# In-projection on rows as they came: gains on w_in, roots on the results, identity products at the start

## The chip, the core and the metric

The kernel runs on one core of one Trainium2 chip. The core has five engines that run side by side: TensorE (PE in the profile; its weight loads are listed as PEld) multiplies matrices, VectorE (DVE), ScalarE (ACT) and GpSimd (POOL) work on elements, and SyncE (SP) only issues transfers. ACT and POOL can issue transfers too; their issues appear as ACTq and POOL rows, those of SyncE as SPq. The metric is the device time of one execution in microseconds; lower is better.

## What is computed

One encoder layer on 1024 tokens of width 1024, in float32. The part that matters here is its beginning:

```python
h = _rmsnorm(x, attn_norm[l])            # x * rsqrt(mean(x*x) + eps) * g
z = h @ w_in[l]                          # 1024 x 1024 times 1024 x 1968
zq, zk, zv, zgate, zg, zcq, zckv, zkpe = jnp.split(z, split_pts, axis=-1)
```

After it come a gated linear attention on zq, zk, zv, zgate with the output gate zg, a latent attention on zcq, zckv, zkpe, an output projection with residual, and an MLP with squared ReLU with residual.

## The kernel before, in words

Every large product is made of float32 operands that are split in two: a high part, rounded to the reduced type fp32r by a copy on ACT, and a low part, which is the value minus its high part. One product is then three matmuls, high by high, high by low and low by high (`split_product`). So each slice of w_in (128 of its 1024 rows, by one group of columns) is transferred into the ring `raw` of four buffers, copied to `wi_hi` by ACT (`in_high_part`), and subtracted into `wi_lo` by DVE (`first_low_part`, the first column group) or POOL (`in_low_part`, the others). Each block of 128 rows of x is transposed on PE against the identity (`norm_T`), copied to `a_hi` by ACT (`norm_hi`), and subtracted into `a_lo` by DVE (`norm_lo`).

The in-projection runs over four groups of columns, q = 0 to 3. Group 0 has 432 columns (latents and gate), groups 1 to 3 have 512 (v, g, and q with k). In each group the eight row blocks b run one after the other, and each takes eight slices k, so 24 matmuls into one of the PSUM banks 0 to 3 (`in_project`). The results leave through DVE (`tile_out`). In group 2, ACT first computes the tanh for the gate.

The norm stands before all of this. ACT sums the squares of a block (`x_square`), POOL makes the root (`x_rstd`), DVE multiplies the block in place by the root and by `gain`, the norm's weights spread over all partitions (`norm_x`, line L1214), and only then does PE transpose it. PE waits for that in `norm_T` (L1756 is its transpose).

The order on each engine is written out by hand, and each engine runs its own list in order. What matters of these lists:

- SP issues the first block of x, then for each slice of group 0 two transfers, one of 416 and one of 16 columns (L456, L461). From the fifth slice on it waits for the low part that frees the ring buffer. For the next group it issues six slices, then the stores of the group (`stores`), and then the last two slices (k = 6 and 7).
- ACT (L957 and on) issues the second block of x, squares block 0, copies slices 0 to 3, issues the third block, copies block 0's transposes, squares block 1, copies slices 4 to 7, issues the fourth block; then for each b it issues one more block, squares block b + 2 and copies the transposes of block b + 1.
- From group to group, ACT and POOL prepare slices 0 and 1 of the next group early, and slices 2 to 7 during the last block. `wi_hi` and `wi_lo` have ten places (`SLICES`), so these six become free one by one as PE passes the last block; in group 2, ACT takes them after the tanh of the last block.
- Between the blocks, `behind(s)` on each engine does the steps of the latent attention's preparation: sums (L914), root (L682), latents transposed (L1827), heads (m_uq, m_ukv), squares (L949), norms, rotary part, transposes of the heads (L1813) and their copies `q_stage` on ACT.

In the profile, most matmuls have the line L1741, most copies of ACT L850, and the low parts of POOL L693.

## Time and profile before

| | before |
|---|---|
| median of 3 runs | 1203.54 us |
| lowest and highest | 1200.26 and 1203.76 us |
| the profiled execution | 1200.04 us, span of its instructions 1198.3 us |
| PE busy | 1160.1 us, 97% of the span |
| DVE, ACT, POOL busy | 780.2, 473.7, 481.4 us |
| mean granted clock of TensorE | 0.991 |
| first product of the in-projection | 12.96 us after the span's start |
| PE waiting for others (view of waits), in all | some 34 us, the longest single wait 9.6 us, at the start |

PE is busy nearly all the time, so what moves the end is only what PE waits for, and how fast its clock is. The profiled execution is a little below the median; a difference of the change is worked out against its rows and put onto the median.

### The profile page before, as it was taken

The numbers are of one execution on the slowest core, as the hardware profiler recorded it, in microseconds if no ns is written. First come the engines' busy times: TensorE is split into PE (matmuls) and PEld (weight loads), VectorE is DVE, ScalarE is ACT, GpSimd is POOL, SyncE is SP. The second block draws the span as 40 slices with busy tenths as digits, with TensorE's granted clock in tenths as the row PEclk, the third lists the DMA queues.
The fourth block names the chain that finished last, engine by engine and source line by source line (L and its number), as shares of the span: only waits on it lengthen the run. The fifth ranks groups of instructions, "written<-read, shape, count | busy, mean of one in ns | idle before, by whom it ended". The sixth has DMA issues, their size and how long they took to land.

```text
span 1198.3 us, 15216 instructions
## 1 busy us (share of the span) xinstructions
PE 1160.1 (97%) x5586; PEld 944.4 (79%) x5586; DVE 780.2 (65%) x1012; ACT 473.7 (40%) x907; POOL 481.4 (40%) x365
## 2 busy tenths in 40 slices
PE   6999999989999999999999999999998999999998
PEld 5967677768878788887788888888876888888887
DVE  5454866535656665137668557865787888888963
ACT  5344534215545555125612233323424334443441
POOL 2442545210000114305844444445435556555652
PEclk9999999999999999999999999999998999999999
DMA  7331342264111103421354342331559785356642
GB/s 239 90 98 62 109 121 87 71 180 172 27 28 43 38 1 114 151 88 71 93 171 141 134 147 94 125 126 62 202 179 357 263 282 192 113 186 210 212 123 88
DMA packets 97353, 158.41 MB, mean 132 GB/s; under 512 B 9024, under 2 KB 38736, under 8 KB 97280
## 3 DMA queue, kind: packets, MB, share of 16 engines
q1 hardware_dynamic: 95728, 152.53, 38.6%
q10 hardware_dynamic: 1008, 3.67, 0.8%
q0 software_dynamic: 544, 1.24, 0.5%
q8 instruction: 45, 0.74, 0.3%
q14 instruction: 28, 0.23, 0.1%
HBM read 115.46 MB, written 41.94 MB: 131 GB/s over the span
## 4 chain that ended last, share of the span: by engine, by line
PE 84%; DVE 8%; issue 3%; ACT 2%; DMA 2%; POOL 1%; SPq 1%; ACTq 0%; DVEq 0%; POOLq 0%
PE ps L1741 79%; PE ps L1961 3%; DVE t_all L1515 1%; DVE g_cum L1305 1%; DVE t_new L1515 1%; PE ps L1756 1%; PE ps L1813 1%; DVE dr_lo L1515 1%; POOL wi_lo L693 1%; DMA gain<-in_attn_norm_dram 1%; DMA up_raw<-in_w_up_dram 1%; DMA r_raw<-in_w_down_dram 1%; ACT q_stage L850 0%; PE ps L1898 0%; DVE a_lo L1515 0%
## 5 line engine op out<-in xcount | busy, mean ns | idle before, releaser
L1741 PE MATMUL ps<-dr_hi,dl_hi 128*128 128x512 f32 x448 | 175.5, 392 | 4.1 <-DVE dr_lo L1515 4.1
L1741 PE MATMUL ps<-dr_hi,dl_lo 128*128 128x512 f32 x448 | 175.3, 391 | 0.0
L1741 PE MATMUL ps<-dr_lo,dl_hi 128*128 128x512 f32 x448 | 175.3, 391 | 0.0
L814 POOL TENSOR_TENSOR ua_lo<-up_raw,ua_hi 128x1024 fp32r<-128x1024 f32 x46 | 116.7, 2539 | 118.1 <-ACT ua_hi L850 118.1
L836 POOL TENSOR_TENSOR dl_lo<-l_raw,dl_hi 128x512 fp32r<-128x512 f32 x64 | 101.6, 1613 | 74.5 <-ACT dl_hi L850 74.0
L1741 PE MATMUL ps<-wi_hi,a_hi 128*128 128x512 f32 (+1 forms) x256 | 105.1, 411 | 3.5 <-POOL wi_lo L693 2.1
L1741 PEld LDWEIGHTS ps<-dr_hi,dl_hi 128*128 128x128 f32 x448 | 84.8, 189 | 22.9 <-issue 3.3
L1741 PE MATMUL ps<-a_hi,ua_hi 128*128 128x512 f32 x256 | 99.9, 390 | 2.0 <-ACT u_two L850 1.8
L836 POOL TENSOR_TENSOR dl_lo<-s_all,dl_hi 128x512 fp32r<-128x512 f32 x48 | 74.7, 1574 | 63.5 <-ACT dl_hi L850 62.6
L1741 PE MATMUL ps<-a_hi,ua_lo 128*128 128x512 f32 x256 | 99.6, 389 | 0.0
L1741 PE MATMUL ps<-a_lo,ua_hi 128*128 128x512 f32 x256 | 99.6, 389 | 0.0
L1741 PE MATMUL ps<-wi_hi,a_lo 128*128 128x512 f32 (+1 forms) x256 | 99.3, 388 | 0.0
L1741 PE MATMUL ps<-wi_lo,a_hi 128*128 128x512 f32 (+1 forms) x256 | 99.2, 388 | 0.0
L1741 PEld LDWEIGHTS ps<-dr_lo,dl_hi 128*128 128x128 f32 x448 | 84.7, 189 | 17.7
L1741 PEld LDWEIGHTS ps<-dr_hi,dl_lo 128*128 128x128 f32 x448 | 84.7, 189 | 17.6
L850 ACT ACTIVATE ua_hi<-up_raw 128x1024 fp32r<-128x1024 f32 x48 | 50.5, 1057 | 87.1 <-PE ps L1741 78.7
L1515 DVE TENSOR_TENSOR dr_lo<-r_raw,dr_hi 128x512 fp32r<-128x512 f32 x64 | 72.5, 1132 | 16.8 <-ACT dr_hi L850 16.7
L1741 PE MATMUL ps<-m_kT,m_qT 96*128 96x512 f32 (+3 forms) x192 | 77.2, 512 | 4.0 <-ACT m_p L1040 4.0
L1741 PE MATMUL ps<-tx_hi,ua_hi 128*128 128x512 f32 x192 | 75.5, 393 | 2.3 <-DVE u_three L1515 2.3
L1741 PE MATMUL ps<-tx_lo,ua_hi 128*128 128x512 f32 x192 | 75.4, 393 | 0.0
L1741 PE MATMUL ps<-tx_hi,ua_lo 128*128 128x512 f32 x192 | 75.2, 392 | 0.0
L850 ACT ACTIVATE dl_hi<-l_raw 128x512 fp32r<-128x512 f32 x64 | 39.8, 622 | 85.3 <-PE ps L1741 83.9
(221 smaller groups left out, 2470.7 us busy)
## 6 DMA issues: line engine op xcount, KB each, us to landing
r_raw<-in_w_down_dram SPq DMA_DIRECT2D x144, 256.0 KB, 3.5
hidden<-stage SPq DMA_DIRECT2D x72, 256.0 KB, 2.0
up_raw<-in_w_up_dram SPq DMA_DIRECT2D x16, 1024.0 KB, 5.6
l_raw<-hidden SPq DMA_DIRECT2D x64, 256.0 KB, 3.4
raw<-in_w_in_dram SPq DMA_DIRECT2D x24, 256.0 KB, 3.0
z_gla<-z_stage SPq DMA_DIRECT2D x16, 256.0 KB, 2.1
raw<-in_w_out_dram SPq DMA_DIRECT2D x16, 256.0 KB, 5.9
xs<-in_x_dram SPq DMA_DIRECT2D x8, 512.0 KB, 8.7
```

What stands on the lines that cost most here:

```text
L693: pool.tensor_tensor(wi_lo[:, n % SLICES, 0:width], raw[:, k % RING, 0:width], wi_hi[:, n % SLICES, 0:width].bitcast(F32), ALU.subtract).t ...
L814: pool.tensor_tensor(ua_lo[n % UP_RING][:, :, :], up_source(g, product), ua_hi[n % UP_RING][:, :, :].bitcast(F32), ALU.subtract).then_inc( ...
L836: pool.tensor_tensor(slot(dl_lo, t), left_source(t), slot(dl_hi, t).bitcast(F32), ALU.subtract).then_inc(dllo_done, 1)
L850: return act.activation(dst, src, ACT.Copy, scale=scale)
L1305: last = dve.tensor_tensor_scan(g_cum[:, t, blk], ones[:, :], g_log[:, t, blk], 0.0, ALU.mult, ALU.add)
L1515: return dve.tensor_tensor(out_, in0, in1, op)
L1741: return pe.matmul(dst, lhsT, rhs, start=start, stop=stop, skip_group_check=onto)
L1756: last = pe.transpose(bank4(4 + j)[:, i, :], src[:, (4 * j + i) * P:(4 * j + i + 1) * P], ident[:, :])
L1813: last = pe.transpose(bank4(4 + i // 4, DQK)[:, i % 4, :], m_qk[:, b % 2, i, :], ident[:, :])
L1961: last = pe.transpose(bank4(4 + c // 4)[:, c % 4, :], m_p[:, i % 2, c * P:(c + 1) * P], ident[:, :])
```

## The change

x is no longer multiplied before it is transposed. The product (x * root * g) @ w is made as root * (x @ (g * w)): the norm's weights multiply the rows of w_in, and the root multiplies each row of the result.

- `gain` spread over the partitions (512 KB) gives way to `gain_col`, 128 by 8, in which each partition has the weights of its own rows; its transfer is issued after the identity is made.
- In group 0, ACT's copy to `wi_hi` takes the weight as its scale, and DVE's low part becomes (raw * gain) - hi in one instruction. In groups 1 to 3, ACT first multiplies the slice in place, waits for that, and then copies it to `wi_hi`; POOL's subtraction is as before.
- DVE's eight `norm_x` go. PE's transposes wait for the block of x alone.
- `tile_out` multiplies by the root, in group 2 through `half_rstd` (half of the root), which also is the scale of the tanh; DVE makes it at the first block of group 1.
- On ACT, the start is reordered: the second block of x is issued only when the first has landed; slices 0 and 1 come first, then block 0's transposes, slices 2 and 3, the squares of block 0, slices 4 to 7, the squares of block 1. DVE's list follows it.
- PE begins with ten products of the identity with itself into bank 3: six before the transposes of block 0 and four behind them. In the first block, PE waits for the first half of `a_lo` before slice 0 and for the second before slice 4.
- Counts of `xn_ready` follow, and POOL's wait for it before four small transfers goes.

```diff
--- before.py
+++ after.py
@@ -36,6 +36,7 @@
 ZM = MLA_W + GR
 
 RING = 4
+WARM_UP = 10
 SLICES = 10
 FT = W // P
 IN_GROUPS, OUT_GROUPS = 4, NH
@@ -227,6 +228,8 @@
         c_rs = small("c_rs", [P, NB, 2])
         h_ss = small("h_ss", [P, 2 * MH])
         h_rs = small("h_rs", [P, 2 * MH])
+        gain_col = small("gain_col", [P, KT])
+        half_rstd = small("half_rstd", [P, NB])
         m_nm = small("m_nm", [P, 2])
         m_sum = small("m_sum", [P, 2, NB])
         m_rden = small("m_rden", [P, NB])
@@ -699,10 +702,10 @@
                 pool.wait_ge(ssq_ready, b + 1)
                 rsqrt(rstd[:, 0, b:b + 1], ssq[:, 0, b:b + 1], D, rstd_ready)
 
-            pool.dma_start(gain[:, :], attn_norm[0].partition_broadcast(P)).then_inc(gain_in, 16)
             step(pool.memset(ident[:, :], 0.0))
             pool.affine_select(out=ident[:, :], in_=ident[:, :], compare_op=ALU.not_equal, fill=1.0, base=0,
                                pattern=[[-1, P]], channel_multiplier=1).then_inc(ident_ready, 1)
+            pool.dma_start(gain_col[:, :], attn_norm[0].rearrange("(k p) -> p k", p=P)).then_inc(gain_in, 16)
             step(pool.memset(minus_half[:, :], -0.5))
             x_rstd(0)
             x_rstd(1)
@@ -722,7 +725,6 @@
             last.then_inc(freq_ready, 1)
             pool.memset(ones[:, :], 1.0).then_inc(ones_ready, 1)
 
-            pool.wait_ge(xn_ready, NB)
             pool.dma_start(gqk[:, 0, :], q_head_norm[0].partition_broadcast(P)).then_inc(phase_in, 16)
             pool.dma_start(gqk[:, 1, :], k_head_norm[0].partition_broadcast(P)).then_inc(phase_in, 16)
             pool.dma_start(gn[:, :], gla_out_norm[0].partition_broadcast(P)).then_inc(phase_in, 16)
@@ -860,7 +862,12 @@
                         act.wait_ge(z_ready, NB * (q0 + 1))
                     else:
                         act.wait_ge(slice_free, (KT - 1) * q0 + k0 + 1)
-                copy(wi_hi[:, n % SLICES, 0:width], raw[:, k % RING, 0:width]).then_inc(whi_done, 1)
+
+                if q:
+                    step(copy(raw[:, k % RING, 0:width], raw[:, k % RING, 0:width], gain_col[:, k:k + 1]))
+                    copy(wi_hi[:, n % SLICES, 0:width], raw[:, k % RING, 0:width]).then_inc(whi_done, 1)
+                else:
+                    copy(wi_hi[:, n % SLICES, 0:width], raw[:, k % RING, 0:width], gain_col[:, k:k + 1]).then_inc(whi_done, 1)
 
             def high_part(q, k):
                 act.wait_ge(raw_in[k % RING], raw_value(q, k))
@@ -955,16 +962,20 @@
                 if s == LOGITS + 2:
                     act.activation(g_cum[:, :, :], g_cum[:, :, :], ACT.Ln, bias=1.0).then_inc(softplus_ready, 1)
 
+            act.wait_ge(x_in[0], 16)
             x_load(1)
+            act.wait_ge(gain_in, 16)
+            for k in range(2):
+                in_high_part(0, k)
+            norm_hi(0, 0)
+            x_load(2)
+            for k in range(2, 4):
+                in_high_part(0, k)
             x_square(0)
-            for k in range(4):
-                in_high_part(0, k)
-            x_load(2)
-            norm_hi(0, 0)
-            x_square(1)
+            x_load(3)
             for k in range(4, KT):
                 in_high_part(0, k)
-            x_load(3)
+            x_square(1)
             for b in range(NB):
                 if b + 4 < NB:
                     x_load(b + 4)
@@ -986,7 +997,8 @@
                         act.wait_ge(z_ready, NB * q + b + 1)
                         if b >= 1:
                             act.wait_ge(z_out, NB * q + b)
-                        act.activation(tanh_g[:, :], ps[:, b % 4, :], ACT.Tanh, scale=0.5).then_inc(tanh_ready, 1)
+                        act.wait_ge(z_out, NB + 1)
+                        act.activation(tanh_g[:, :], ps[:, b % 4, :], ACT.Tanh, scale=half_rstd[:, b:b + 1]).then_inc(tanh_ready, 1)
                     if q + 1 < IN_GROUPS and b in (0, NB - 1):
                         for k in range(0, 2) if b == 0 else range(2, KT):
                             in_high_part(q + 1, k)
@@ -1110,7 +1122,7 @@
                 if n < UP_RING:
 
                     act.wait_ge(x2_stored[n], 32)
-                    act.wait_ge(xn_ready, NB + 2 * n + 2)
+                    act.wait_ge(xn_ready, 2 * n + 2)
                 else:
                     act.wait_ge(part_ready, 2 * (n - UP_RING + 1))
                 if product in (P1, P4):
@@ -1253,24 +1265,28 @@
                 q, b = divmod(s, NB)
                 dve.wait_ge(z_ready, s + 1)
                 tile = ps[:, s % 4, :]
+                root = rstd[:, 0, b:b + 1]
                 n = s - NB
                 if 2 <= n < 2 * NB:
                     dve.wait_ge(z_stored[n % 2], 16 * (n // 2))
                 if q == 0:
-                    dve.tensor_copy(zm[:, b, :], tile[:, 0:ZM]).then_inc(z_out, 1)
+                    dve.wait_ge(rstd_ready, b + 1)
+                    dve.tensor_scalar(zm[:, b, :], tile[:, 0:ZM], root, None, ALU.mult).then_inc(z_out, 1)
                 elif q == 1:
-                    dve.tensor_copy(z_stage[:, n % 2, :], tile).then_inc(z_out, 1)
+                    if b == 0:
+                        dve.tensor_scalar(half_rstd[:, :], rstd[:, 0, :], 0.5, None, ALU.mult)
+                    dve.tensor_scalar(z_stage[:, n % 2, :], tile, root, None, ALU.mult).then_inc(z_out, 1)
                 elif q == 2:
 
                     dve.wait_ge(phase_in, 64)
                     dve.wait_ge(tanh_ready, b + 1)
                     step(stt(z_stage[:, n % 2, :], tanh_g[:, :], 1.0, tile, ALU.add, ALU.mult))
                     g4 = z_stage[:, n % 2, :].rearrange("p (h v) -> p h v", h=GH)
-                    stt(g4, g4, 0.5, gn[:, :].unsqueeze(1).broadcast_to([P, GH, GDV]), ALU.mult, ALU.mult).then_inc(z_out, 1)
+                    stt(g4, g4, half_rstd[:, b:b + 1], gn[:, :].unsqueeze(1).broadcast_to([P, GH, GDV]), ALU.mult, ALU.mult).then_inc(z_out, 1)
                 else:
 
                     dve.wait_ge(cum_ready, GT)
-                    dve.tensor_copy(zqk[:, b, :], tile).then_inc(z_out, 1)
+                    dve.tensor_scalar(zqk[:, b, :], tile, root, None, ALU.mult).then_inc(z_out, 1)
 
             def head_norms(b):
 
@@ -1339,20 +1355,16 @@
 
             def first_low_part(k):
                 dve.wait_ge(whi_done, k + 1)
-                dve.tensor_tensor(wi_lo[:, k, 0:ZM], raw[:, k % RING, 0:ZM], wi_hi[:, k, 0:ZM].bitcast(F32),
-                                  ALU.subtract).then_inc(wlo_done, 1)
+                stt(wi_lo[:, k, 0:ZM], raw[:, k % RING, 0:ZM], gain_col[:, k:k + 1], wi_hi[:, k, 0:ZM].bitcast(F32),
+                    ALU.mult, ALU.subtract).then_inc(wlo_done, 1)
 
             dve.wait_ge(gain_in, 16)
-            norm_x(0, 0, x0, x0[:, 0, :])
-            for k in range(RING):
+            for k in range(2):
                 first_low_part(k)
             norm_lo(0, 0)
-            norm_x(0, 1, x0, x0[:, 1, :])
-            for k in range(RING, KT):
+            for k in range(2, KT):
                 first_low_part(k)
             for b in range(NB):
-                if b + 2 < NB:
-                    norm_x(0, b + 2, x0, x0[:, b + 2, :])
                 if b + 1 < NB:
                     norm_lo(0, b + 1)
                 tile_out(b)
@@ -1747,7 +1759,7 @@
                 return mm(dst, lo, rhs_hi, False, last, onto)
 
             def norm_T(r, b, src):
-                pe.wait_ge(xn_ready, NB * r + b + 1)
+                pe.wait_ge(x_in[b], 16)
                 for j in range(2):
                     n = 2 * (NB * r + b) + j
                     if n >= 2:
@@ -1763,6 +1775,8 @@
                 if n >= 4:
                     pe.wait_ge(z_out, n - 3)
                 for k in range(KT):
+                    if n == 0 and k % 4 == 0:
+                        pe.wait_ge(alo_done, k // 4 + 1)
                     if between is not None and k == KT // 2:
                         between()
                     if b == 0:
@@ -1862,11 +1876,16 @@
 
 
             pe.wait_ge(ident_ready, 1)
-            norm_T(0, 0, x0[:, 0, :])
+
+            for n in range(WARM_UP):
+                if n == WARM_UP - 4:
+                    norm_T(0, 0, x0[:, 0, :])
+                mm(ps[:, 3, 0:P], ident[:, :], ident[:, :], True, True)
             for b in range(NB):
                 if 1 <= b < NB - 1:
                     norm_T(0, b + 1, x0[:, b + 1, :])
-                pe.wait_ge(alo_done, 2 * b + 2)
+                if b:
+                    pe.wait_ge(alo_done, 2 * b + 2)
                 in_project(0, b, (lambda: norm_T(0, 1, x0[:, 1, :])) if b == 0 else None)
                 behind(b)
             for q in range(1, IN_GROUPS):
@@ -2021,7 +2040,7 @@
 
 
             def norm_T2(pos):
-                pe.wait_ge(xn_ready, NB + pos + 1)
+                pe.wait_ge(xn_ready, pos + 1)
                 if pos >= 2:
                     pe.wait_ge(xt_free, pos - 1)
                 elif pos == 0:
```

## Rows read from the trace of the kernel before

**Rows 1.** Timeline at the start: start us, duration us, engine, line, operation, out<-in, [idle before]

```profile
1.29 0.75 POOL L702 DMA_DIRECT2D gain<-in_attn_norm_dram  x1 [0.80 <-POOLq L2131]
2.52 0.29 POOL L704 TENSOR_SCALAR_AFFINE_SELECT ident<-ident 128x128 f32<-128x128 f32 x1 [0.25 <-POOL ident L703]
5.59 1.03 ACT L876 ACTIVATE ps<-x 128x1024 f32<-128x1024 f32 x1 [3.08 <-DMA x<-in_x_dram]
8.18 1.28 DVE L1214 SCALAR_TENSOR_TENSOR x<-x,rstd,gain 128x1024 f32<-128x1024 f32 x1 [8.18 <-DMA gain<-in_attn_norm_dram]
8.34 2.23 ACT L850 ACTIVATE wi_hi<-raw 128x432 fp32r<-128x432 f32 x4 [1.60 <-DMA raw<-in_w_in_dram]
```

**Rows 2.** Chain that ended last, in order of time: start us, length us, what

```profile
12.96 4.69 PE ps L1741 x12
22.52 4.71 PE ps L1741 x24
```

**Rows 3.** Busy time by stretch, PE alone: stretch, us, PE busy, granted clock, DMA share, GB/s

```profile
13.00:14.00 1.00, 1.00 (x3) 1.00 1.04 376
```

**Rows 4.** DMA issues of the first 30 us: KB each, us from issue to landing

```profile
gain<-in_attn_norm_dram POOLq DMA_DIRECT2D x1, 512.0 KB, 6.9
places<-in_positions_dram POOLq DMA_DIRECT2D x1, 4.0 KB, 3.1
```

**Rows 5.** Timeline between blocks 0 and 1 of group 0

```profile
13.22 0.64 SPq L461 DMA_DIRECT2D raw<-in_w_in_dram  x1
14.30 2.38 ACT L850 ACTIVATE wi_hi<-raw 128x432 fp32r<-128x432 f32 x4 [1.08 <-DMA raw<-in_w_in_dram]
17.04 1.03 ACT L876 ACTIVATE ps<-x 128x1024 f32<-128x1024 f32 x1 [0.36 <-issue]
20.34 1.28 DVE L1225 TENSOR_TENSOR a_lo<-ps,a_hi 128x512 fp32r<-128x512 f32 x2
```

**Rows 6.** PE's timeline: the latents' products, in plain float32

```profile
65.46 2.74 PE L1741 MATMUL ps<-m_uq,m_cT 128*128 128x384 f32 x8
```

**Rows 7.** PE's timeline after a long wait late in the kernel

```profile
875.75 0.67 PE L1741 MATMUL ps<-tx_hi,ua_hi 128*128 128x512 f32 x1 [2.26 <-DVE u_three L1515]
```

**Rows 8.** Busy time by stretch, PE alone, in the same place

```profile
875.00:880.00 5.00, 4.25 (x12) 0.66 0.83 276
```

**Rows 9.** Timelines of ACT, POOL and PE from group 0 to group 1

```profile
55.80 2.39 ACT L850 ACTIVATE wi_hi<-raw 128x512 fp32r<-128x512 f32 x4 [4.70 <-PE ps L1741]
56.51 7.54 POOL L693 TENSOR_TENSOR wi_lo<-raw,wi_hi 128x512 fp32r<-128x512 f32 x6 [4.57 <-ACT wi_hi L850]
62.00 0.63 ACT L850 ACTIVATE wi_hi<-raw 128x512 fp32r<-128x512 f32 x1 [0.84 <-DMA raw<-in_w_in_dram]
64.78 0.39 PE L1741 MATMUL ps<-wi_hi,a_hi 128*128 128x512 f32 x1
```

**Rows 10.** Timelines of DVE and PE after the first block of group 1

```profile
65.66 0.69 DVE L1262 COPY z_stage<-ps 128x512 f32<-128x512 f32 x1 [5.20 <-PE ps L1741]
77.22 0.52 PE L1827 MATMUL ps<-ident,zm 128*128 128x128 f32 x3 [1.82 <-ACT v_stage L850]
```

**Rows 11.** Groups of DVE, shapes apart: busy us, mean ns | idle before

```profile
L1326 DVE TENSOR_SCALAR g_log<-ps,bg 128x512 f32<-128x512 f32 x4 | 3.0, 750 | 0.3
```

**Rows 12.** Timelines of ACT and PE in the first blocks of group 2

```profile
148.37 1.30 ACT L850 ACTIVATE wi_hi<-raw 128x512 fp32r<-128x512 f32 x2 [0.68 <-DMA raw<-in_w_in_dram]
151.01 0.60 ACT L989 ACTIVATE tanh_g<-ps 128x512 f32<-128x512 f32 x1 [1.34 <-DVE z_stage L1214]
152.72 0.52 PE L1827 MATMUL ps<-ident,zm 128*128 128x128 f32 x3 [1.12 <-ACT q_stage L850]
```

**Rows 13.** Timelines of ACT, POOL and PE from group 2 to group 3

```profile
200.51 2.18 ACT L850 ACTIVATE wi_hi<-raw 128x512 fp32r<-128x512 f32 x4
201.21 7.99 POOL L693 TENSOR_TENSOR wi_lo<-raw,wi_hi 128x512 fp32r<-128x512 f32 x6 [2.19 <-ACT wi_hi L850]
209.25 0.50 PE L1741 MATMUL ps<-wi_hi,a_hi 128*128 128x512 f32 x1 [0.17 <-POOL wi_lo L693]
```

## The prediction, made before the change was run

> **What bounds the kernel now.** PE is busy 97% of the span, so I read the view of PE's waits first, for what it waits for at all, then the timelines of all engines at its longest wait, then the chain of work that ended last, which says which of those waits carry to the end. Everything the change touches lies in the first 210 us; the projections and the MLP behind it only move along with it.
>
> The longest wait is the first. The rows to see: the weights of the norm, spread over all partitions, are issued at 1.29 and let DVE start at 8.18 us [rows 1]; the first block of x had landed by 5.59. DVE's multiplication (1.28 us), PE's transposes, ACT's copy and DVE's low part follow one another, and the chain reaches the first product at 12.96 [rows 2]. The twelve products of 432 columns from there take 4.69 us, the 24 of the second block 4.71 [rows 2]: 0.39 against 0.20 us each. The granted-clock column reads 1.00 in that stretch [rows 3], but 432 columns in 0.39 us (with the first one's start-up) is the lower level, 1.2 GHz, and 0.20 the upper, 2.4, so I go by the distances here. The second block's products begin at 22.52 on the chain. From there on PE has work without a gap until the groups change, so **the change's worth at the start is the move of that 22.52**, not of 12.96.
>
> **The start, part by part.** Removed: 512 KB of spread weights, the 1.28 us of DVE, and the second block of x out of the first transfers, 1 MB of the 2.4 MB of the first transfers (two blocks of x, four slices, the weights). Added: gain_col, 4 KB in pieces of one element. The nearest row is the positions' transfer, the same 128 by 8 of four-byte values: 3.1 us to landing [rows 4]; the spread weights took 6.9. The identity is made first; it was ready at 2.52 + 0.29 = 2.81 behind an issue of 0.75 [rows 1], so at about 2.1 now, and gain_col is issued then: landed between 2.1 + 3.1 = 5.2 and 2.1 + 6.9 = 9.0. Slice 0 was complete at 8.34 [rows 1]; with 1 MB less at 376 GB/s [rows 3] it comes up to 2.8 us earlier, at 5.5. I take 6.2 as the time S at which ACT can start, near to the slice and to the positions' row, which is the same transfer; its end at 5.5 and, with half the distance to the spread weights' row, 7.4 bound this case, and 9.0 is a rival of its own below.
>
> From S in ACT's new order, with copies of 0.56 (2.23 / 4 [rows 1]) for slices and about 0.55 for transposes: slices 0, 1 to S + 1.1, both halves of block 0 to S + 2.2, one issue, slices 2, 3 to S + 3.7, DVE's low parts of 0.6 behind, the last at S + 4.4. The first product is at about S + 2.6 = 8.8, 4.2 us earlier than 12.96. But slice 7's buffer is freed by that last low part. Before, its last issue stood at 13.22, and its copy, the fourth of 2.38 us from 14.30, began by 16.1 and ended at 16.68 [rows 5]: 2.9 us from issue to copy at most. Now the last issue stands at about S + 5.2 (0.9 for the two), the copy begins at S + 8.1 and ends at S + 8.6 = 14.8.
>
> Behind slice 7 stands what I think decides: before, ACT had squared block 1 earlier; from 16.68 it issued two blocks, squared block 2 (17.04 [rows 5]) and copied block 1's transposes, DVE's low parts of these ended at 20.34 + 1.28 = 21.62 [rows 5], and the product came at 22.52, 0.9 later, with transposes between. Now the squares of block 1 stand in this line too. Counted: squares of block 1 and 2, 2 x 1.25 (1.03 [rows 5] and 0.2 for reading the sum); one issue 0.36; two halves 1.1; the last low part 0.8; then 0.9: 5.7 us. Block 1 starts at 14.8 + 5.7 = 20.5. **Gain 2.0 us**; with S at its bounds 2.7 and 0.8. Squares, roots (POOL) and x's later blocks are hidden: x's third block is issued at about S + 2.5 and isn't squared before S + 10.
>
> **The clock.** The ten identity products: the latents' float32 products show as eight rows of 384 columns in 2.74 us [rows 6], two rows for each matmul, so 0.69 us for 384 columns and 0.23 for 128 at full clock, 0.46 at half. Six cost 1.4 to 2.8 us from 2.1 on, over before or just as x lands; the other four end by 9 at the latest. They are covered by the wait for slice 0 and cost nothing; without that cover they would cost 2.3 to 4.6. They may well save the 0.19 us on each of the twelve slow products. But block 0 then waits for slices 4 to 7, which come no faster, so that saving isn't on the path: it is nothing of the sum. What counts is the clock when block 1 begins. Between the last product of block 0 (slice 7's low part, then three products: 14.8 + 1.3) and the next transposes (14.8 + 4.2) lie **2.9 us without work for PE, wherever S is**. The nearest row is the wait of 2.26 us before 875.75 [rows 7], behind which the granted clock averages 0.66 over 5 us [rows 8]: (1 - 0.66) / 0.5 x 5 = 3.4 us at the lower level, 1.7 us of work lost. Before, PE had no such gap here. Bounds: nothing if the clock holds, 2.8 if it comes back as slowly as at the start, where twelve products lost 12 x 0.19 = 2.3 us [rows 2] and the transposes behind them some more. I take **+1.7 us**, the nearest row's. The Trainium skill (TensorE: Matmul & The Clock Gate, "What's actually happening") says that the throttled state is the default and that activity lifts it, and in "HAM oscillation" that idle gaps between bursts bring it back: by the first the identity products pay, by the second the gap behind block 0 takes it back. The rows at the start and at 875.75 agree with each.
>
> **The changes of group.** In groups 1 to 3, each slice needs two passes of ACT instead of one, the second waiting for the first. The nearest rows: four copies in 2.39 us [rows 9], two in 1.30 [rows 12]; so 0.60 to 0.65 for a pass and 1.20 to 1.30 for the pair. POOL's low parts take 7.54 / 6 = 1.26 [rows 9] and 7.99 / 6 = 1.33 [rows 13]. So ACT becomes just as slow as POOL, and only the pair of the first slice and the second pass of the last stick out.
> - Group 0 to 1: POOL's last low part ended at 56.51 + 7.54 = 64.05; slice 7 came by transfer at 62.00 [rows 9]. Its buffer is free 0.6 later (the first pair), it lands 0.6 later, and its pair takes 0.6 more: low part at 65.3. PE wants it at 64.78 [rows 9]: +0.5.
> - First block of group 1: its result opens DVE's rotary steps (65.66 [rows 10]), at whose end PE waits 1.82 us (77.22 [rows 10]). half_rstd costs 0.2 and the multiplication 0.75 [rows 11] instead of 0.69: +0.3 on this path.
> - Group 1 to 2: the low parts are late here for another reason (DVE and POOL behind the scans), so the pairs hide up to slice 7. But behind it, ACT's heads are 0.65 later, so their store, so the two next slices that SP issues behind it (148.37 [rows 12]); with their two pairs ACT is free at about 151.6 and not before the tanh at 151.01, for whose q_stage PE waits 1.12 us (152.72 [rows 12]): +0.65, bounds 0 and 1.4.
> - Group 2 to 3: ACT starts at 200.51, POOL at 201.21, and PE waits for the last, 209.25 [rows 13]. First pair and second pass of the last: +1.1, and ACT's next copies for PE +0.15; bounds 0.65 and 1.5.
> - The other results of DVE: 24 times 0.06 us and POOL's freed wait are hidden; PE has four banks.
>
> Sum of these: +2.7, bounds 1 and 4. The whole: -2.0 + 1.7 + 2.7 = **+2.4 us**. The profiled execution's own 1200.04 becomes 1202.4; it lies 3.5 below the median, and against the median of 1203.54 the forecast is **1205.9**.
>
> **The rivals.**
> - The clock holds over the gap. For it: PE is not quite idle before it, and the identity products end close to the first product. Then -2.0 + 2.7 = +0.7: 1204.2.
> - Faster: the start pays in full. gain_col lands at 5.2, ACT's pairs hide behind POOL except at one change of group, and the clock holds: -2.7 + 1.0 = -1.7. If slice 7's copy also comes 2 to 3 us sooner after the start than before, -4 to -5: 1198.5 to 1201.8. Against it: slice 7 hangs on the ring, not on traffic.
> - Slower: ACT becomes the bound at the changes of group. It decides as soon as a pair takes longer than POOL's 1.26 to 1.33. At 1.5 us, five more slices at two changes cost 0.2 each, +2.0; at 1.6, +3.0: with the clock lost, 1207.9 to 1208.9. At 1.3 or less, none of it. For it: two full passes with a wait between are at that edge already.
> - gain_col as the new wait, as the first product was held by gain before. One element for each piece; at 6.9 us as the spread weights, S is 9.0, and block 1 starts at 23.3 instead of 22.52, so +0.8 in place of -2.0: 1208.7. The Trainium skill (DMA: Bandwidth & Descriptors, "Rules for kernel authors") says of a non-contiguous last dimension that it is one descriptor per element and should be rearranged; that speaks for this one. The positions' row at 3.1 us speaks against it.
> - The identity products don't raise the clock. Then block 0 runs at half; its last product comes later, the gap shrinks, and block 1 starts up to 1 us later: 1204.5 to 1206.9, inside the range.
>
> **How the numbers follow.** Forecast with the clock lost 0.37; clock holds 0.24; faster 0.18; ACT as the bound 0.11; gain_col late 0.05; identity without effect 0.05. A measurement of this kernel can tell about 0.3% from no change, 3.6 us: below 1199.9 or above 1207.2. Faster by that is most of the third case: 0.14. Slower by that: the fourth and fifth cases and the upper part of the first, 0.24. The same: 0.62. The range goes from 1199.5, inside the faster rival, to the slower one's 1208.9.
>
> **What would show it.** In the profile after: PE's first rows are identity products at about 2; ACT's first copy ends its wait at 5.6 to 7.4, and what released it says whether gain_col or slice 0 was last; the first product near 8.8; the copy of slice 7 ends near 14.8; block 1's first product at 20.5 by my count, with a gap of about 2.9 us before its transposes, and products at 0.36 (432 columns at 1.2 GHz) instead of 0.20 us behind it if the clock went. ACT's pairs at 1.2 to 1.3 us; POOL's last low part of groups 1 and 3 about 1.1 us later against the block it follows. What would make it wrong: slice 7 landing well before S + 8, a clock that stays up, or pairs longer than 1.35 us.

## The result

The changed kernel takes 1208.8 us (median of 7, 1206.0 to 1211.1) where the kernel before, on the same chip, takes 1200.9 (median of 7): a ratio of 1.0065 with an interval of 1.0047 to 1.0083, so **7.8 us slower**. The forecast was slower by 2.4; the time lies at the upper end of the range, and the sign of the sum was right, but its size was a third of what happened. That the time lies inside the range is luck: the forecast was put onto a median of three runs, 1203.5, and the seven here have 1200.9. As a difference the range went up to +5.4, and 7.8 lies beyond it. The profiled execution took 1210.2 us, with a span of 1208.5, 10.2 more than before.

The page of the kernel after: span, then for each engine busy time, share of the span and instructions.

```profile
span 1208.5 us, 15282 instructions
PE 1170.4 (97%) x5606; PEld 951.1 (79%) x5606; DVE 771.4 (64%) x1005; ACT 491.3 (41%) x931; POOL 481.2 (40%) x365
```

PE is busy 10.3 us longer. Some 4.5 us of that are the ten identity products (a row of 2.93 us is shown below, a second one took 1.87), which lie where PE stood idle before; the other 5.8 us come with the same products as before, so much of the loss hides in the busy time, where a slower clock lies. The mean granted clock is 0.984 (0.991 before). Where it arises, the chain of work shows. First rows of before that did not stand ahead of the prediction (start us, length us, what), then those of after in the same places.

```profile
28.10 4.71 PE ps L1741 x24
50.42 9.40 PE ps L1741 x48
77.74 0.87 PE ps L1852 x8
104.76 0.89 PE ps L1813 x8
122.69 1.76 PE ps L1813 x16
168.52 0.89 PE ps L1813 x8
```

```profile
10.02 5.99 DMA raw<-in_w_in_dram
16.03 1.21 ACT wi_hi L852 x2
21.51 1.94 PE ps L1768 x8
23.45 5.41 PE ps L1753 x24
29.73 4.69 PE ps L1753 x24
52.03 5.31 PE ps L1753 x27
80.65 0.87 PE ps L1866 x8
109.24 0.89 PE ps L1827 x8
127.16 1.76 PE ps L1827 x16
142.49 3.76 DMA raw<-in_w_in_dram
149.65 8.04 PE ps L1753 x27
175.62 0.89 PE ps L1827 x8
217.91 0.96 PE ps L1753 x3
```

After minus before, place by place: block 1 of group 0 +0.9 (22.52 stands in [rows 2]), block 2 +1.6, the end of group 0 +1.6, the first heads +2.9, 104.76 against 109.24 +4.5, 122.69 against 127.16 +4.5, the middle of group 2 +7.1, the last slice of group 3 +8.7 (209.25 in [rows 13]), the end +10.2. So the profiled difference is 1.6 at the start, 1.3 from group 0 to 1, 1.6 between 80 and 109 us, 2.6 from group 1 to 2, 1.6 from group 2 to 3, and 1.5 in the remaining 990 us.

**The start.** PE's timeline (start us, duration us, engine, line, operation, out<-in, count, idle before and who ended it):

```profile
1.58 2.93 PE L1753 MATMUL ps<-ident 128*128 128x128 f32 x12 [1.58 <-POOL ident L706]
9.81 0.47 PE L1753 MATMUL ps<-wi_hi,a_hi 128*128 128x432 f32 x1 [1.82 <-DVE a_lo L1237]
17.44 0.46 PE L1753 MATMUL ps<-wi_hi,a_hi 128*128 128x432 f32 x1 [1.82 <-DVE wi_lo L1226]
18.55 0.56 PE L1753 MATMUL ps<-wi_lo,a_hi 128*128 128x432 f32 x1
18.91 0.56 PE L1753 MATMUL ps<-wi_hi,a_lo 128*128 128x432 f32 x1
21.51 1.94 PE L1768 MATMUL ps<-ident,x 128*128 128x128 f32 x8 [0.96 <-DVE a_lo L1237]
```

ACT's timeline:

```profile
7.12 0.65 ACT L852 ACTIVATE wi_hi<-raw,gain_col 128x432 fp32r<-128x432 f32 x1 [0.66 <-DMA gain_col<-in_attn_norm_dram]
13.35 0.66 ACT L852 ACTIVATE wi_hi<-raw,gain_col 128x432 fp32r<-128x432 f32 x1 [1.81 <-DMA raw<-in_w_in_dram]
16.03 1.84 ACT L852 ACTIVATE wi_hi<-raw,gain_col 128x432 fp32r<-128x432 f32 x3 [2.02 <-DMA raw<-in_w_in_dram]
```

ACT starts at 7.12, the first product stands at 9.81, 3.2 us earlier than 12.96. But slice 5 lands at 16.01 (10.02 + 5.99 on the chain), 6 and 7 right behind it, and slice 7's copy ends at 17.87, where it ended at 16.68 before [rows 5]. From there to block 1 it is 5.6 us, 1.1 of them because the eight transposes take 1.94 instead of 0.87 us.

**From group 1 to 2.** ACT and POOL of after, and DVE between them:

```profile
146.27 0.72 ACT L852 ACTIVATE raw<-raw,gain_col 128x512 f32<-128x512 f32 x1 [1.14 <-DMA raw<-in_w_in_dram]
147.73 1.86 POOL L696 TENSOR_TENSOR wi_lo<-raw,wi_hi 128x512 fp32r<-128x512 f32 x1 [1.19 <-ACT wi_hi L852]
146.74 1.73 DVE L1295 TENSOR_TENSOR m_qk<-m_qk,h_rs 128x1536 f32<-128x1536 f32 x1
149.65 0.50 PE L1753 MATMUL ps<-wi_hi,a_hi 128*128 128x512 f32 x1 [2.09 <-POOL wi_lo L696]
```

The same four in the kernel before:

```profile
140.94 0.63 ACT L850 ACTIVATE wi_hi<-raw 128x512 fp32r<-128x512 f32 x1 [1.08 <-DMA raw<-in_w_in_dram]
137.89 5.48 POOL L693 TENSOR_TENSOR wi_lo<-raw,wi_hi 128x512 fp32r<-128x512 f32 x4
142.21 2.78 DVE L1279 TENSOR_TENSOR m_qk<-m_qk,h_rs 128x1536 f32<-128x1536 f32 x1
143.42 0.50 PE L1741 MATMUL ps<-wi_hi,a_hi 128*128 128x512 f32 x1 [0.39 <-POOL wi_lo L693]
```

This is the largest single term, and it is **a step, not a slope**. Before, POOL makes four low parts without a pause until 143.37; DVE's multiplication of the heads, ready at 142.21, takes 2.78 us since it stands behind the last of them. After, slice 7 has landed later (3.76 us behind its issue) and needs two passes; POOL is idle for 1.19 us, DVE's multiplication slips in and runs its 1.73 us until 148.47, and POOL's low part, begun at 147.73, ends 1.1 us behind that. PE's wait is 2.09 us instead of 0.39. And behind it the clock falls. PE alone, by stretch (us, PE busy, granted clock, DMA share, GB/s):

```profile
150.00:155.00 5.00, 5.00 (x16) 0.66 0.73 246
```

A mean of 0.66 over 5 us is 3.4 us at 1.2 GHz: 1.7 us of work lost, on top of 1.7 of waiting; of these 3.4, 0.8 are taken back from the later waits. Two things make slice 7 late here: it landed 0.8 us later behind its issue than before (3.76 against 2.96), and it has the second pass. The second run below shows that the pass alone is enough to open the gap.

### The profile page after: what moved, and what is told of

It reads as the page before. It is cut to its first block, busy times and chain, and to the rows that moved or that the text cites. A ratio compares the mean times of both kernels' runs of the same rounds, so it can differ in the third digit from the quotient of the medians.

```text
span 1208.5 us, 15282 instructions
## 1 busy us (share of the span) xinstructions
PE 1170.4 (97%) x5606; PEld 951.1 (79%) x5606; DVE 771.4 (64%) x1005; ACT 491.3 (41%) x931; POOL 481.2 (40%) x365
## 4 chain that ended last, share of the span: by engine, by line
PE 83%; DVE 6%; DMA 3%; issue 3%; ACT 2%; POOL 2%; SPq 1%; ACTq 0%; DVEq 0%; POOLq 0%
PE ps L1753 77%; PE ps L1980 3%; DMA raw<-in_w_in_dram 1%; DVE t_all L1527 1%; POOL wi_lo L696 1%; PE ps L1827 1%; DVE t_new L1527 1%; DVE dr_lo L1527 1%; DMA up_raw<-in_w_up_dram 1%; DMA r_raw<-in_w_down_dram 1%; PE ps L1768 1%; DMA gain_col<-in_attn_norm_dram 0%; ACT wi_hi L852 0%; SPq L617 0%; DVE rk L1246 0%
```

## Experiments

Each ratio is against runs of the kernel before on the same chip (medians 1199.6 to 1200.3); times put against each other are ratios times 1200. The intervals are 3.1 to 4.4 us wide, so a difference of 1 us between two kernels is not shown by their times.

### The pass taken out

```diff
                 if q:
-                    step(copy(raw[...], raw[...], gain_col[:, k:k + 1]))
                     copy(wi_hi[...], raw[...]).then_inc(whi_done, 1)
```

> The changed kernel without the pass that multiplies a slice in place in groups 1 to 3: one copy as before. Left out: the norm's weights in groups 1 to 3, so only group 0 is computed in full. Theory (the loss behind the start is ACT's second pass at the changes of group, 0.7 us on each first and last slice, plus transfers that wait for them): the stretches from block 7 of group 0 to the first result of group 1, and the waits before groups 2 and 3, go back to those of before; 3.5 to 5 us less than the changed kernel's 1208.8, so about 1204 to 1205. Rival A (the start alone is the loss, the groups only show noise): no difference from 1208.8 beyond 1 us. Rival B (the roots' multiplications in the results cost it): no difference either, and the waits for POOL's low parts stay.

Ratio 1.0025 (1.0012 to 1.0038): of 7.8 us, 4.8 are gone. The clock does not fall near 150 us, the wait for the last slice there is 0.38 again. Where the remaining 3.0 us lie, its profile tells only in part: it is the fastest of the 12 runs, block 1 stands at 21.97, 0.55 ahead of before, and the span is only 0.9 longer. The other runs had a lower clock (below), and no trace says where.

### The pass alone, added to before

```diff
+                if q:
+                    step(copy(raw[:, k % RING, 0:width], raw[:, k % RING, 0:width]))
                 copy(wi_hi[...], raw[...]).then_inc(whi_done, 1)
```

> The kernel before the change with one thing added: an in-place copy of each slice on ScalarE ahead of its high part in groups 1 to 3 (with no scale; nothing is left out, the results are those of before). Theory 1 (the pass costs what leaving it out of the changed kernel brought, 4.8 to 6 us, whatever the start does): 1199.9 + 5.3 = about 1205.2, block 1 unchanged at 22.5 us, and a half-level stretch between 140 and 155 us. Theory 2 (about half of the 6 us comes from its meeting a start that is earlier or later): 1202 to 1203. The pass without a scale operand should take about 0.60 instead of 0.72 us, so the pair 1.16, below GpSimd's 1.26, and the cost may come out up to 1 us lower for that.

Ratio 1.0044 (1.0026 to 1.0062), 5.3 us. Taken out or put in, the pass costs the same within the noise, so most of its price does not depend on the start. The profiled execution is 4 us above the median of its runs. Block 1 stands at 22.50, and the step of the change from group 1 to 2 is there, with the clock behind it. PE's timeline:

```profile
149.38 0.50 PE L1743 MATMUL ps<-wi_hi,a_hi 128*128 128x512 f32 x1 [2.09 <-POOL wi_lo L693]
```

PE by stretch, the columns as above:

```profile
150.00:155.00 5.00, 5.00 (x17) 0.66 0.77 243
```

Here slice 7 landed only 1.7 us behind slice 6, as before; the pass alone was enough to open the gap of 0.43 us on POOL into which DVE's 1.73 us went.

### The pass only for group 2

```diff
-                if q:
+                if q == 2:
                     step(copy(raw[...], raw[...], gain_col[:, k:k + 1]))
+                    copy(wi_hi[...], raw[...]).then_inc(whi_done, 1)
+                elif q:
                     copy(wi_hi[...], raw[...]).then_inc(whi_done, 1)
```

> The changed kernel with the in-place scaling only for the slices of group 2; the norm's weights are left out of groups 1 and 3, so the output differs there. The kernel without any of the three passes takes 1202.5. Theory 1 (at the change from group 1 to 2 the pass lengthens TensorE's wait to about 2.1 us, and the clock falls behind it): a stretch of 3.4 us or more at the half level begins between 143 and 151 us, which the kernel without the pass doesn't have, and the time is 2.6 us longer: 1205.1. Theory 2 (the loss there needs the delays of the other two passes too): the waits there stay at 1.2 us, the clock holds, 1203.

Ratio 1.0033 (1.0015 to 1.0051), 1203.6 us. The signs of theory 1 are there: a wait of 2.77 us for the last slice, and 6.8 us at the half level from 143 on; between 120 and 171 us its profile loses 4.7 us against before. But the wait is not the step described above: slice 7 landed 5.15 us behind its issue, and DVE's multiplication came behind POOL as before (2.76 us). The median is only 1.0 us above that without any pass, not 2.6. One profile shows only part of why: the clock did not fall between 90 and 110 us in it, where it falls in every other one. In time, this run is inconclusive.

### The scaling earlier

```diff
-                    step(copy(raw[...], raw[...], gain_col[...]))
+                    if not 2 <= k < 6:
+                        step(copy(raw[...], raw[...], gain_col[...]))
...
+            def scale_early(q):
+                for k in range(2, 6):
+                    act.wait_ge(raw_in[k % RING], raw_value(q, k))
+                    step(copy(raw[...], raw[...], gain_col[...]))
...
+                if b == NB - 2:
+                    scale_early(1)
...
+                    if q + 1 < IN_GROUPS and b == NB - 2:
+                        scale_early(q + 1)
```

> The changed kernel, but the in-place scaling of slices 2 to 5 of the next group's weights is done one block earlier (behind block 6), where ScalarE has time; nothing is left out. Slices 0, 1, 6 and 7 keep the pair of passes. Theory 1 (the loss at a change of group is the pair of the first slice and the second pass of the last): the pair of slice 2 is off the path, 0.75 us at each of three changes of group, about 2.2 us in all: 1206.5. Theory 2 (ScalarE's total is what costs there, since four pairs in a row at 1.28 us keep pace with GpSimd's 1.26): more than that comes back, near the 4.8 us that leaving out the pass brought: 1203 to 1204.5. Theory 3 (what is gained is taken by the last two slices, whose landing sets the end): under 1 us, 1208 to 1208.8.

Ratio 1.0069 (1.0056 to 1.0083): nothing gained in time, as theory 3 had it, but its profile does not bear out theory 3's reason. Two changes of group became shorter. From the first block of group 1 to the second it was 0.9 us less than in the change, and from ACT's first slice for group 3 to PE's last one 1.0 less: 9.25 us here, 10.22 in the change, 8.74 before. ACT's first slice in the change, then ACT's first slices and PE's last one here:

```profile
207.69 0.71 ACT L852 ACTIVATE raw<-raw,gain_col 128x512 f32<-128x512 f32 x1
208.43 2.18 ACT L852 ACTIVATE wi_hi<-raw 128x512 fp32r<-128x512 f32 x4
217.68 0.50 PE L1763 MATMUL ps<-wi_hi,a_hi 128*128 128x512 f32 x1 [0.78 <-POOL wi_lo L696]
```

So the first pair of a change of group was on the path. What was won there went elsewhere: from group 1 to 2 slice 7 landed 4.9 us behind its issue (3.76 in the change) and PE waited 3.07 us, and the clock fell once more, at 79 us.

### The squares behind the copy

```diff
-            x_square(1)
             for b in range(NB):
                 if b + 4 < NB:
                     x_load(b + 4)
-                if b + 2 < NB:
-                    x_square(b + 2)
                 if b + 1 < NB:
                     norm_hi(0, b + 1)
+                if b == 0:
+                    x_square(1)
+                if b + 2 < NB:
+                    x_square(b + 2)
```

> The changed kernel with ACT's squares of blocks 1 and 2 moved behind the copies of block 1's transposes. Theory (these two squares, 2.4 us, stand on the path between slice 7's copy and block 1): block 1's first product at 23.1 - 2.4 = 20.7, PE's gap before it near 0.5 to 1 us instead of 3 us, and the clock may hold there; in all 2 to 3.5 us less than the changed kernel, about 1206. Rival (the slices' landing or DVE sets block 1, and the squares lie beside it): block 1 stays within 0.5 us of 23.1, time unchanged.

Ratio 1.0058 (1.0039 to 1.0076), 0.8 us better than the change, which is within the noise. Block 1 moved from 23.45 to 19.88: this is the path from slice 7 to block 1 as the prediction counted it. But only a part arrives: its profile loses 4.6 us against before at the change from group 1 to 2, 2.0 more than the change does, with slice 7 landing 4.9 us behind its issue, a wait of 3.08 us and 6.8 us at the half level.

### The fourth block of x later

```diff
             x_square(0)
-            x_load(3)
             for k in range(4, KT):
                 in_high_part(0, k)
+            x_load(3)
```

> The changed kernel, but the fourth block of x (512 KB) is issued only behind the copies of slices 4 to 7, as before the change; nothing is left out. Theory 1 (the block shares the DMA engines with slices 4 to 7 and makes them land late): the copy of slice 7 ends at about 16.2 instead of 17.87, block 1's first product comes 1.5 us earlier, at about 21.6, and the kernel takes 1.5 us less: 1207.3. Theory 2 (the late landing is the transfers' own latency with their many queued pieces, not this block): slice 7's copy stays within 0.5 us of 17.87, the time within 0.5 us of 1208.8.

Ratio 1.0062 (1.0047 to 1.0077). The copy of slice 7 ended at 16.00. Seven profiles have the change's order of transfers at the start; there it ended between 16.76 and 17.87, in the mean at 17.2. In the three with the fourth block later (this one and two below) it was 14.97, 15.83 and 16.00, mean 15.6. The landing shows it more closely: slice 7 was complete 4.0 to 4.9 us behind its last issue in the seven and 2.6 to 2.9 in the three. So theory 1 holds for the landing; of the time, 0.4 us came, which is within the noise. The gap ahead of block 1's transposes was longer here than in the change (0.96), and the clock stayed, as PE's timeline and its stretch show:

```profile
19.64 1.16 PE L1768 MATMUL ps<-ident,x 128*128 128x128 f32 x8 [2.02 <-DVE a_lo L1237]
```

```profile
17.00:22.00 5.00, 2.98 (x18) 1.00 1.01 376
```

### No products of the identity

```diff
-            for n in range(WARM_UP):
-                if n == WARM_UP - 4:
-                    norm_T(0, 0, x0[:, 0, :])
-                mm(ps[:, 3, 0:P], ident[:, :], ident[:, :], True, True)
+            norm_T(0, 0, x0[:, 0, :])
```

> The changed kernel without the ten identity products. Theory (block 0 waits for slices 4 to 7, whatever the clock does): products of block 0 at 0.36 us from the start on, block 1's first product within 0.7 us of 23.1, time within 1 us of the changed kernel's. Rival A (the identity products do buy the clock for block 0): block 1's first product 2 us or more later, time 2 to 3 us longer. Rival B (they harm, by bringing the fall of the clock into block 0): 1 to 2 us shorter.

Ratio 1.0063 (1.0045 to 1.0082), that of the change (1.0065). Neither a help nor a cost shows.

### The identity products in the kernel before

```diff
             pe.wait_ge(ident_ready, 1)
-            norm_T(0, 0, x0[:, 0, :])
+            for n in range(20):
+                if n == 14:
+                    norm_T(0, 0, x0[:, 0, :])
+                mm(ps[:, 3, 0:P], ident[:, :], ident[:, :], True, True)
```

> The kernel before, with nothing but 20 identity products, 14 ahead of block 0's transposes and 6 behind them. In the kernel before, block 0's first twelve products and the eight transposes run at the lower level and are on the path to block 1 (22.25 in the timeline). Theory: with the clock up at 12.96, they take 2.3 + 0.8 us less, block 1's products start at 20 to 20.5, and the time is 2 to 3 us below that of before: about 1198.5. Rival (slices 4 to 7 or ACT's copies of block 1's transposes are next late): block 1 moves by less than 1 us, time as before.

Ratio 1.0032 (1.0017 to 1.0046): slower by 3.8 us, where I expected a gain. Its products of block 0 do run at 2.4 GHz, and it is of no use. Timelines of DVE and PE, then PE by stretch:

```profile
19.14 1.28 DVE L1214 SCALAR_TENSOR_TENSOR x<-x,rstd,gain 128x1024 f32<-128x1024 f32 x1 [1.85 <-POOL rstd L682]
21.17 1.16 PE L1756 MATMUL ps<-ident,x 128*128 128x128 f32 x8 [2.77 <-DVE a_lo L1225]
```

```profile
22.00:27.00 5.00, 5.00 (x21) 0.66 0.73 247
```

Block 1 hangs on ACT and DVE: DVE multiplies block 2 by the norm ahead of block 1's low parts. That row stood in before as well (its low parts at 20.34 in [rows 5]) and I had not seen what it stood behind. Faster products only open a gap of 2.77 us, and the clock falls behind it, as the prediction described it for another kernel. That is 1.4 of the 4.6 us by which its profile is longer; 1.7 more come up to 138 us, where the clock stood at the half level for 6.8 us near 100 instead of 3.4.

### The gap ahead of block 1 filled

```diff
+                if b == 1:
+                    for n in range(FILL):        # FILL = 10
+                        mm(ps[:, 3, 0:P], ident[:, :], ident[:, :], True, True)
                 if 1 <= b < NB - 1:
                     norm_T(0, b + 1, x0[:, b + 1, :])
```

> The changed kernel with ten more products of the identity (128 columns each) between the last product of block 0 and the transposes ahead of block 1; nothing is left out. Those transposes stand at 21.51 us after about 1.2 us of idle TensorE and the products behind them run at 0.36 us, the half level, until the clock has come back. Theory 1 (the gap costs the clock): filled, the products of block 1 run at 0.20 us, block 1's first product stays at about 23.1, block 2's first comes at about 28.5 instead of 29.7, and the kernel takes about 1 to 1.5 us less, 1207.5. Theory 2 (the level at the start is not set by this gap): the products behind it stay at 0.36, and the time is that of the changed kernel, 1208.8, or up to 1 us more, since the added products delay the transposes.

Ratio 1.0065 (1.0050 to 1.0079), no gain. In its profile the products around the gap run at 0.20 us each, and block 2 starts at 27.58 instead of 29.73. But the last products of block 0, ahead of the filling, run at 0.20 us already: the fall of the clock at 18 us that the change's profile has was not there to be cured, so this run does not decide between the two theories. The profile has one fall of the clock more at 79 us, and it is the fastest of its runs; the median is that of the change.

### All three edits, and the same without the pass

```diff
             x_square(0)
-            x_load(3)
             for k in range(4, KT):
                 in_high_part(0, k)
-            x_square(1)
+            x_load(3)
...
+                if b + 1 < NB:
+                    norm_hi(0, b + 1)
+                if b == 0:
+                    x_square(1)
                 if b + 2 < NB:
                     x_square(b + 2)
-                if b + 1 < NB:
-                    norm_hi(0, b + 1)
```

With all three, scale_early from above is added; without the pass, the line with step(copy(raw, raw, gain_col)) is taken out instead.

> The changed kernel with three edits together: the squares of blocks 1 and 2 behind the copy of block 1's transposes, the scaling of slices 2 to 5 one block earlier, and the fourth block of x behind the copies of slices 4 to 7; nothing is left out. If the three act on separate stretches their gains add: -1.9 (squares, measured), -2.2 (scales) and -1.5 (fourth block) from 1208.8 give 1203.2, still above the 1200.3 of the kernel before. Rival: time gained at the start and at one change of group opens a longer wait at the next one, as the squares' edit already showed (2.6 us won up to the second group, 1.9 in the end): 1205 to 1206.

> The changed kernel with the two edits of the start (squares behind the copy of block 1's transposes, fourth block of x later) and without the in-place pass; the norm's weights are left out of groups 1 to 3. It asks what the start is worth when nothing else differs from before at the changes of group. Block 1's first product should stand at about 17.8 us as with all three edits, 4.2 us before that of the kernel without the pass (21.97), which takes 1202.5. Theory 1 (time won at the start stays won where no pass follows): 1202.5 - 4.2 = 1198.3, 1.5 to 2 us under the kernel before. Theory 2 (the slices at the change from group 1 to 2 land 3.8 to 4.3 us after their issue instead of 3.0 whenever the phase of the stores differs from that of before, TensorE waits 2 us there, the clock falls behind it): 2.4 us are given back between 122 and 171 us, with 3.4 us or more at the half level starting between 135 and 150 us, and the time is 1200.5 to 1201.5.

Ratios 1.0042 (1.0029 to 1.0056) and 1.0001 (0.9988 to 1.0014). The difference, 4.9 us, is the price of the pass a third time (here with four of the scalings made one block earlier). With all three, 1205.1 us, the rival held (1205 to 1206): the gains don't add. The second is the point of the case: block 1 stands at 18.67 us, 3.9 earlier than before, and at 119.15 it is still 3.5 us ahead of before's 122.69; at 167.56 it is only 1.0 ahead of 168.52. Its chain, then PE's timeline and PE by stretch:

```profile
119.15 1.76 PE ps L1827 x16
134.47 4.38 DMA raw<-in_w_in_dram
141.63 8.02 PE ps L1753 x27
167.56 0.89 PE ps L1827 x8
```

```profile
141.63 0.74 PE L1753 MATMUL ps<-wi_hi,a_hi 128*128 128x512 f32 x1 [2.09 <-POOL wi_lo L696]
```

```profile
140.00:144.00 4.00, 2.37 (x6) 0.72 0.24 75
```

Without the pass, slice 7 landing 4.4 us behind its issue instead of some 3.0 opened the same gap, and 2.6 us went, as theory 2 put it (1200.5 to 1201.5; it was 1200.6).

### The weights of the norm on the transposed x

The low parts on DVE take the weights in the same way, and the start has the order of the kernel with all three edits.

```diff
-                    copy(a_block(a_hi, slice(4 * j, 4 * j + 4), b), bank4(4 + j)).then_inc(ahi_done, 1)
+                    for i in range(4):
+                        k = 4 * j + i
+                        last = copy(a_block(a_hi, k, b), bank4(4 + j)[:, i, :], gain_col[:, k:k + 1])
+                    last.then_inc(ahi_done, 1)
...
-                    step(copy(raw[...], raw[...], gain_col[:, k:k + 1]))
```

> A kernel that computes the whole with the norm's weights in another place: neither on x's rows nor on the slices, but on the transposed x, where they are one number for each partition: ScalarE's copies of the transposes and VectorE's low parts take them as an operand, eight pieces of 128 columns for each block instead of two of 512. The slices need no scaling, so the second pass is gone; the order of the start is that of the kernel with all three edits. The eight pieces cost ScalarE about 8 x 0.27 = 2.2 us instead of 1.1 for each block and VectorE perhaps 2 instead of 1.3; both have room in group 0 except ahead of block 1. Theory: block 1's first product at 17.8 + 1.1 + 0.6 = 19.5 us, 3 us before that of the kernel before; the changes of group as before the change; in all 1199.9 - 3 = 1197. Rival: the pieces of block 0 and 1 lie in a chain with slices 4 to 7 and delay them, block 1 at 21 to 22, and the time is that of before, 1199 to 1200.

Ratio 1.0047 (1.0032 to 1.0063): 2.2 us better than the change, which is at the edge of the noise, and 5.6 slower than before. Eight pieces took 2.18 us on ACT and 2.16 on DVE, block 1 came at 21.03, 1.5 ahead of before, and at the change from group 1 to 2 the step is there again: slice 7 landed 3.1 us behind slice 6, PE waited 2.09, 3.4 us ran at the half level. Neither of my two accounts held in time; no kernel here beats the one before.

### Where the time is, over all runs

Each run lists its time and mean granted clock; time x clock is about what it would have taken at full clock, the rest is lost to the lower level. Means over runs:

| kernel | runs | time x clock | lost |
|---|---|---|---|
| before | 81 | 1189.9 to 1190.6 | 9.2 to 10.2 |
| change | 7 | 1192.2 | 16.9 |
| one_pass | 12 | 1189.5 | 13.3 |
| pass_alone | 12 | 1193.3 | 12.4 |
| all_three | 11 | 1189.8 | 15.2 |
| start_without_pass | 12 | 1186.6 | 13.8 |
| scaled_transposes | 12 | 1189.9 | 15.6 |
| scales_early | 5 | 1190.0 | 18.9 |

The clock is given to 0.001, 1.2 us. Two things more bend this split. The twelve slow products at the start of before and the transposes behind them, some 3 us of lost work, show no lower clock in the record, so they stand in its time x clock and not under lost. And a stretch at the half level counts as lost also where PE had to wait anyway, as in the change's profile between 11.3 and 14.5 us (granted clock 0.50), ahead of the slices 5 to 7. Place by place the change's profile gives, of its 10.2 us, 5.1 to the clock (1.8 at the start, 1.6 between 80 and 109 us, 1.7 behind 150), 3.6 to waits, and leaves 1.5 open. With that said: **of the change's loss, the waits make 2 to 4 us and the clock the larger part**. By the table start_without_pass wins 3.5 us beside the clock and returns 3.7 in it, and scales_early wins 2.2 us against the change and returns 2.0.

## Why the prediction came out as it did

- **What bounds the start; S (when ACT can start), first product.** Right in kind. S was 7.1 (6.2, bound 7.4; half way between the two rows is 7.1, not 7.4): gain_col took 5.36 us to land, between the two rows; the first product came at 9.8 (8.8), S + 2.7 where S + 2.6 was counted.
- **The path from slice 7 to block 1.** 5.6 us (5.7), but partly by luck: 1.1 of it is the slow transposes, which the prediction had in its term for the clock. Where the clock held, in one_pass, the path was 4.8 us; moving the squares off it showed that it is the path.
- **Slice 7's copy at 14.8.** Wrong by 3.1 us, and with it the gain of 2.0. 0.9 of this is S. The failed step is "2.9 us from issue to copy at most": the issue stood at 12.32, S + 5.2 as counted, but slices 5 to 7 landed 4.9 to 6.0 us behind their issues, slice 7 at 17.20, which is 2.0 us over the 2.9. The change issues x's fourth block ahead of them, and I had not counted its 512 KB on the DMA engines; in the three runs with it later slice 7 landed 2.6 to 2.9 us behind its issue, as the prediction had it. The last 0.2 us is the copy itself, 0.65 instead of 0.5.
- **The clock at the start, +1.7.** The size was right: transposes 1.94 instead of 0.87 and 24 products 5.41 instead of 4.71, 1.8 us. The cause was not, so the size is luck: the products were slow from 18.2 on, before the gap, which was 0.96 us and not 2.9. Behind the longer gap of 2.02 or 2.03 us in four other runs (third_block_later, one_pass, no_identity, pass_into_group_2) nothing fell, and of the seven profiles with the change's order of transfers only two, the change's and that of scales_early, have the fall near 18 us at all. What sets it off is open. The Trainium skill (TensorE: Matmul & The Clock Gate, "HAM oscillation") says that idle gaps between bursts bring the throttled state back; of the gaps of 2 to 3 us here, those near 145 us and the one of 2.77 in before_identity agree, those of 2.02 and 2.03 don't.
- **Group 0 to 1, +0.8.** It was 1.3: 0.75 at the last slice (0.5 counted) and 0.55 behind it (0.3). The pair took 1.28 us as bounded, so ACT as the bound did not come true. The first pair makes the last slice late, as counted: with the scaling earlier PE did not wait for that slice at all (0.53 us in the change).
- **Group 1 to 2, +0.65 with a bound of 1.4.** The worst step, 2.6. "The pairs hide up to slice 7" was right; I then followed the wrong branch, the heads and q_stage (the wait there became shorter, not longer), and put no price on slice 7's own 0.7 us. I read the row of PE's wait (0.39 us) as slack that grows by what is added. It is a step: a late slice lets DVE's 1.73 us in ahead of POOL, and the wait of 2.1 us that follows costs the clock.
- **Group 2 to 3, +1.25.** 1.6. Right: the first pair does count, 1.0 us by the earlier scaling, and the rest lies at the last two slices, for which PE waited 0.53 and 0.84 us.
- **Between 80 and 109 us.** Not in the sum: 1.6 us, the clock at the half level for 6.8 instead of 3.4 us, near 100 us. It is so in the change, pass_alone, all_three, scales_early, third_block_later and no_identity, all with the pass, but also in before_identity, without it, and not in squares_behind and gap_filled, with it. In five kernels with the pass (pass_alone, scales_early, no_identity, gap_filled, all_three) it also fell for 3.4 us between 76 and 80 us. What decides there is open.
- **Identity products.** Nothing, as forecast.

The sum of terms was -2.0 + 1.7 + 2.7. With the sizes measured, it is +1.6 at the start (its clock included), +5.5 at the changes of group, +1.6 between, and 1.5 in the rest of the kernel, for which no run has an account.

## What to carry to other kernels

An addition to a chain that has slack is not priced by the slack alone: ask which other engine's instruction stands ready behind it and will run first once the chain is late (here DVE's against POOL's), and add what it then takes; and read what the granted clock does behind each wait. Time won early on was given back at the first place where an order of two engines had been just right; compare time x clock and time lost to the clock beside the medians, which mix them. A pass that only keeps pace with its neighbour still costs at the first item of a ring and at the last ones. And an edit that leaves the time as it was may have won in one place and lost in another: read the places before calling it idle.

## What the runs showed of the hardware that I had not expected

- **DVE and POOL take turns.** DVE's multiplication of 128 by 1536 took 1.73 us with POOL idle at its start and 2.76 to 2.78 us when it began during a low part of POOL; POOL's low part took 1.4 us by itself and 1.8 to 2.8 when it began during that multiplication, ending 1.1 us behind it each time. In the eight kernels where it did (the change, pass_alone, no_identity, gap_filled, third_block_later, all_three, start_without_pass, scaled_transposes) PE's wait at this place was 2.08 to 2.10 us, whether POOL began 0.3 or 1.3 us after its last low part: the length of DVE's instruction sets it. In the three where slice 7 came later still (4.9 to 5.2 us behind its issue) the landing sets it, and the wait was 2.77 to 3.08 us. The Trainium skill (SBUF — State Buffer, "Who interferes with whom") says that a DVE instruction with two inputs in SBUF contends with a GpSimd one that reads SBUF, and that the one that issues first has the shared ports for its whole length. The trace agrees; by the rule the turn could have been foreseen from before's 2.78, though not the lateness that brings it about.
- **A transfer's landing varies by some 2 us with something outside the ring.** Slice 7 of group 2 landed 2.8 to 5.2 us behind its issue. It landed 1.7 to 1.9 us behind slice 6 in before, before_identity, pass_alone, no_identity and gap_filled. In these traces no packet of the instruction queue (0.02 MB) lies between its issue and its landing. In scaled_transposes, start_without_pass, pass_into_group_2, scales_early, squares_behind, third_block_later, all_three and the change there is one, and it was 2.1 to 3.8 us; the store of z behind it then took 4.1 to 5.4 us to land instead of 3.1 to 3.4. One_pass has the packet and 1.9 us. The two go together in thirteen of the fourteen traces; that the packet is the cause was not tested.
- **A copy on ACT with a scale from a tile** took 0.65 us for 432 columns where one with a constant took 0.56; the in-place pass of 512 columns 0.71 against 0.62. Less of it shows in a row of copies, since one begins before the other ends: a pair of passes took 1.28 against 1.19 us.
- **gain_col, 4 KB in single elements**, landed after 5.36 us on POOL's queue in the change, after 4.6 to 5.6 in the other kernels that have it.
